# Three low parts per down stage move from a ScalarE copy and an accumulating transfer to one VectorE subtraction

## The reference

```
h = h + jnp.concatenate([y_lru, y_att], axis=-1) @ w_out[i]
u = rmsnorm(h, ln_ffn[i])
g_up, v_up = jnp.split(u @ w_up[i], 2, axis=-1)
g_up = causal_dwconv(g_up, ffn_conv_w[i], ffn_conv_b[i])
h = h + (jax.nn.gelu(g_up) * v_up) @ w_down[i]
gate = jax.nn.sigmoid(rmsnorm(h, ln_ple[i]) @ w_ple_gate[i])
h = h + gate * (p[i].astype(h.dtype) @ w_ple_proj[i])
```

## Time and profile before

| what | value |
|---|---|
| median of three runs | 634.01 us (633.53 to 634.43) |
| profiled execution, device time | 634.09 us |
| its span, first to last instruction | 632.3 us |
| TensorE | busy 627.9 us |
| VectorE | busy 438.4 us |
| ScalarE | busy 337.3 us |
| GpSimd | busy 362.1 us |
| granted TensorE clock | 1.000 |
| transfers of the software queue (only L563's) | 1296 packets, 4.72 MB |

### The profile page before, as it was taken

How to read it: one execution, slowest core, us unless ns; L and a number is a source line. 1 busy time by engine, 2 the same in 40 slices (tenths; PEclk the granted TensorE clock), 3 DMA queues, 4 the chain that set the end, 5 groups by cost and what they waited for, 6 DMA issues and landing times.

```text
span 632.3 us, 7947 instructions
## 1 busy us (share of the span) xinstructions
PE 627.9 (99%) x2885; PEld 521.5 (82%) x2885; DVE 438.4 (69%) x650; ACT 337.3 (53%) x492; POOL 362.1 (57%) x267
## 2 busy tenths in 40 slices
PE   9999999999999999999999999999999999999997
PEld 7887788888888888888888888888888888888886
DVE  3692499978748797769734477697354677989574
ACT  5779953878836455546333345453343364457341
POOL 6684433743307537499664454996644559963370
PEclk9999999999999999999999999999999999999999
DMA  8742335471103644303546223045462222652022
GB/s 297 289 136 98 101 100 133 123 203 61 41 1 121 242 171 167 100 1 102 132 137 233 97 100 101 1 119 128 154 230 76 99 95 93 170 172 100 34 84 83
DMA packets 22934, 77.80 MB, mean 123 GB/s; under 512 B 2672, under 2 KB 3184, under 8 KB 22640
## 3 DMA queue, kind: packets, MB, share of 16 engines
q1 hardware_dynamic: 21456, 72.45, 34.3%
q0 software_dynamic: 1296, 4.72, 4.0%
q10 hardware_dynamic: 144, 0.13, 0.1%
HBM read 64.83 MB, written 4.19 MB: 109 GB/s over the span
## 4 chain that ended last, share of the span: by engine, by line
PE 99%; DVE 0%; issue 0%; POOL 0%; POOLq 0%
PE psum L1519 30%; PE psum L1521 30%; PE psum L1520 30%; PE psum L1715 2%; PE psum L1701 1%; PE psum L1661 1%; PE psum L1565 1%; PE psum L1568 1%; PE psum L1573 1%; PE psum L1598 1%; PE psum L1848 1%; PE psum L1631 1%; PE psum L1616 1%; PE psum L1682 0%; PE psum L1558 0%; PE psum L1658 0%
## 5 line engine op out<-in xcount | busy, mean ns | idle before, releaser
L505 POOL TENSOR_TENSOR wlo<-raw,whi 128x512 fp32r<-128x512 f32 x82 | 112.9, 1377 | 192.3 <-ACT whi L591 191.9
L1521 PE MATMUL psum<-uhi,wlo 128*128 128x512 f32 x488 | 189.8, 389 | 0.0
L1520 PE MATMUL psum<-ulo,whi 128*128 128x512 f32 x488 | 189.8, 389 | 0.0
L1519 PE MATMUL psum<-uhi,whi 128*128 128x512 f32 x488 | 189.8, 389 | 0.0
L506 POOL TENSOR_TENSOR wlo<-raw,whi 128x512 fp32r<-128x512 f32 x82 | 117.6, 1434 | 0.0
L591 ACT ACTIVATE whi<-raw 128x1024 fp32r<-128x1024 f32 x78 | 81.9, 1054 | 58.0 <-PE psum L1521 57.3
L1520 PEld LDWEIGHTS psum<-ulo,whi 128*128 128x128 f32 x488 | 91.6, 188 | 19.1
L1519 PEld LDWEIGHTS psum<-uhi,whi 128*128 128x128 f32 x488 | 91.6, 188 | 19.1
L1521 PEld LDWEIGHTS psum<-uhi,wlo 128*128 128x128 f32 x488 | 91.6, 188 | 18.9
L837 ACT ACTIVATE tmp<-psum,vec 128x512 f32<-128x512 f32 x24 | 16.6, 690 | 84.3 <-DVE psum L1293 84.3
L1364 DVE TENSOR_TENSOR ws<-raw,held 128x1024 f32<-128x1024 f32 x24 | 47.1, 1987 | 9.3 <-POOL elo L557 9.1
(11 more groups left out here) (253 smaller groups left out, 1183.9 us busy)
## 6 DMA issues: line engine op xcount, KB each, us to landing
raw<-in_weights SPq DMA_DIRECT2D x94, 512.0 KB, 3.3
held<-in_weights SPq DMA_DIRECT2D x12, 512.0 KB, 5.7
wlo<-ws POOLq DMA_DIRECT2D x6, 512.0 KB, 5.9
xtok<-in_x SPq DMA_DIRECT2D x4, 512.0 KB, 8.8
out<-first SPq DMA_DIRECT2D x1, 2048.0 KB, 8.7
back<-out SPq DMA_DIRECT2D x1, 2048.0 KB, 7.7
first<-in_x_t SPq DMA_DIRECT2D x7, 256.0 KB, 7.1
raw<-in_weights SPq DMA_DIRECT2D x7, 256.0 KB, 7.1
```

Source lines behind the costliest of these rows:

```text
L505: nc.gpsimd.tensor_tensor(wlo[s][:, 0:CW // 2], raw[s][:, 0:CW // 2], whi[s][:, 0:CW // 2].bitcast(F32), ALU.subtract)
L1519: mm(o, ahi, bhi, start=start, stop=False, skip_group_check=shared)
L1520: mm(o, ahi, blo, start=False, stop=False, skip_group_check=shared)
L1521: return mm(o, alo, bhi, start=False, stop=stop, skip_group_check=shared)
```

## The change

The negated copy on ScalarE, the accumulating transfer and its semaphores go. A new helper own_low on VectorE subtracts the high part from the sum in ws for units 8, 10 and 12 and counts v_low. All that waited for x_low waits for v_low. VectorE's order changes: the three subtractions are put in, and sum 6 moves behind give 0.

```diff
             for ph in range(PHASES):
...
                 for u in range(N_UNITS):
-                    if u in ADDED:
-                        unit_add(ph, u)
-                    else:
+                    if u not in OWN:
                         unit_low(ph, u)
...
                 nc.scalar.activation(high[:, :], whole[:, :], ACT.Copy).then_inc(d_hi, 1)
-                if u in ADDED:
-                    act.wait_ge(d_hi, N_UNITS * ph + u + 1)
-                    nc.scalar.activation(low[:, :], high[:, :].bitcast(F32), ACT.Copy, scale=-1.0).then_inc(d_neg, 1)
...
                 elif n == 9:
-                    dve.wait_ge(x_low[8], 16 * (ph + 1))
+                    dve.wait_ge(v_low, len(OWN) * ph + 1)
...
+            def own_low(ph, u):
+
+                high, low = unit_slot(u)
+                dve.wait_ge(d_hi, N_UNITS * ph + u + 1)
+                V.tensor_tensor(low[:, :], ws[SUM_AT[SUM_UNITS.index(u)]][:, :], high[:, :].bitcast(F32), ALU.subtract).then_inc(v_low, 1)
...
+                own_low(ph, 8)
+                give(ph, 0)
                 weight_sum(ph, 6)
-                give(ph, 0)
                 weight_sum(ph, 7)
                 give(ph, 1)
+                own_low(ph, 10)
                 weight_sum(ph, 8)
                 weight_sum(ph, 9)
                 give(ph, 2)
+                own_low(ph, 12)
                 give(ph, 3)
                 give(ph, 4)
...
-                if u in ADDED:
-                    pe.wait_ge(x_low[u], 16 * (ph + 1))
+                if u in OWN:
+                    pe.wait_ge(v_low, len(OWN) * ph + OWN.index(u) + 1)
```

More of the change, by code:

```diff
@@ L136 @@
 PRODUCT_UNITS = [UNITS.index((o, 1)) + 1 for o in range(7)]
-ADDED = (8, 10, 12)
-LOW_UNITS = N_UNITS - len(ADDED)
+OWN = (8, 10, 12)
+LOW_UNITS = N_UNITS - len(OWN)
 SUM_UNITS = [u for u, (o, _) in enumerate(UNITS) if PRODUCTS[o][2] is not None]
@@ L163, in lows_upto @@
 def lows_upto(ph, u):
-    return LOW_UNITS * ph + u + 1 - sum(x < u for x in ADDED)
+    return LOW_UNITS * ph + u + 1 - sum(x < u for x in OWN)
 def after_down(c):
@@ L343, in build @@
         y_copy = sem("y_copy")
-        w_sum, d_hi, d_neg, d_lo, d_step = (sem(n) for n in ("w_sum", "d_hi", "d_neg", "d_lo", "d_step"))
-        x_low = {u: sem(f"x_low{u}") for u in ADDED}
+        w_sum, d_hi, v_low, d_lo, d_step = (sem(n) for n in ("w_sum", "d_hi", "v_low", "d_lo", "d_step"))
         unit_done, res_moved = sem("unit_done"), sem("res_moved")
@@ L558, in unit_low @@
                                         ALU.subtract).then_inc(d_lo, 1)
[L560 to L564, removed]
             for ph in range(PHASES):
@@ L835, in tap_up @@
                     else:
-                        act.wait_ge(x_low[12], 16 * (f // 8))
+                        act.wait_ge(v_low, len(OWN) * (f // 8))
                 nc.scalar.activation(ytile[f % 4], up_bank(f, 0), ACT.Identity, bias=0.0,
@@ L891, in square_ple @@
                 elif m == 0:
-                    act.wait_ge(x_low[12], 16 * PHASES)
+                    act.wait_ge(v_low, len(OWN) * PHASES)
                 elif m == 2:
@@ L1356, in weight_sum @@
                 elif n == 9:
-                    dve.wait_ge(x_low[8], 16 * (ph + 1))
+                    dve.wait_ge(v_low, len(OWN) * ph + 1)
                 elif ph and n == 0:
-                    dve.wait_ge(x_low[10], 16 * ph)
+                    dve.wait_ge(v_low, len(OWN) * ph)
                 elif ph:
```

## The result

| kernel | median us | runs | ratio to before, 95% interval |
|---|---|---|---|
| before | 633.97 | 633.53 to 634.43 (4) | |
| the change | 637.06 | 636.78 to 638.48 (4) | 1.0052 (1.004 to 1.0064) |

The change costs 3.1 us where 2.7 were forecast. The profiled execution is the slowest of the four (638.48 us, span 636.7): in it TensorE's clock fell for some microseconds after the longer wait. The other three lie between 636.8 and 637.2 us with spans of 635.0 to 635.4. One execution of the kernel with seven memsets (see the experiments) took 698.6 us at a mean granted clock of 0.851 and is left out of its numbers.

A forecast was written before the change was run, and what follows sets the result against it. TensorE, busy 99% of the span, bounds the kernel. Span 632.3 plus 2.7 us lateness at turn_back(4) gives 635.0; with 1.8 us around the span, 636.7 us against 634.01; range 634.4 to 638.6, forecast case's own 636.2 to 637.2.

The forecast's parts named there:

- What bounds: Whole span: TensorE is busy 99% and waits once, 1.0 us at the start; nothing the change removes stands on the path.
- Phases 0 and 1 covered: Phases 0 and 1: give 5 ends at 442.6, the next up tile comes at about 445.2; cover 2.6 us, no loss.
- The three subtractions: VectorE, phase 2: own_low(8), (10), (12) take 2.24, 1.35 and 1.22 us, cost 4.81; VectorE is 3.49 us late after give 4.
- the rival at 638.2: GpSimd goes first at own_low(12), where the margin is 0.21 us; add_back(0) starts 4.2 us late, 638.2 us; chance 20%.
- sharing at half speed: VectorE and GpSimd share SBUF at half speed instead of excluding each other: about +3.0 in place of +2.7 us; no chance given.
- pTlo blocked: VectorE, phase 2: the pTlo pair from 565.28 meets GpSimd's halves, lasts 3.0 us, not 1.29; add_back(0) at 568.19, 2.7 us late.
- From add_back(0) to give 6 as a block: Phase 2: everything from add_back(0) to give 6 moves together, so give 6 and turn_back(4) are 2.7 us late.
- The waits: TensorE waits twice after its start, near 564.8 (turn_back(0), about 0.8 us) and 575.4 (turn_back(4), about 1.9 us).
- The rival that the gap takes it: VectorE's 2.42 us gap before add_back(0) absorbs lateness, pTlo finding GpSimd idle: 635.1 us, or 634.0 at free pace; chance 17%.
- The rival that it gets faster: The 1.8 us around the span partly belong to the software queue and go; with no wait 632.2 us; chance 7%.

The follow-up runs named there:

- the kernel with seven memsets: The kernel before with seven memsets of acc on VectorE between give 4 and the pTlo pair of phase 2: 639.90 us, ratio 1.0089.
- The versions without the transfers and with no wait of TensorE: Give 6 ahead of low_ple, with the change plus pTlo on GpSimd and phase 2's own_low(12) behind give 4 (634.36 us), or all low parts on GpSimd (634.29).
- The kernel that holds GpSimd back: The changed kernel, with GpSimd waiting for the pTlo pair before the low part of the next stage's first chunk: 636.14 us, ratio 1.0035.
- The padded kernel: The kernel before with four memsets of acc on VectorE between give 4 and the pTlo pair of phase 2: 635.62 us, ratio 1.0025.

## Why the prediction was right, and where it was off

- **What bounds.** Right: no time came from what was removed. The versions without the transfers and with no wait of TensorE take the time of the kernel before (634.36 and 634.29 against 634.30).
- **Phases 0 and 1 covered.** Right, by the kernel with the change in these alone. Give 5 in phase 1 ended at 442.33 (forecast 442.6), the up tile came at 444.95 (445.2).
- **The three subtractions.** 2.31, 1.42 and 1.30 us, with 2.24, 1.35 and 1.22 forecast from start to start (544.07 to 546.31, 553.19 to 554.54, 560.30 to 561.52: 2.24, 1.35, 1.22). Give 3 was forecast at 561.70 and started at 561.52, which is 561.68 in the other execution's frame. own_low(12) won its turn, so the rival at 638.2 did not come; unit 13's second half took 2.28 us behind it. The prediction also named sharing at half speed, with about +3.0, which by the number alone is nearer to 3.1. These rows rule it out: own_low(12) had halves beside it all the time and at half speed would have taken, by estimate, nearly twice its free 1.13 us; it took 1.22.
- **pTlo blocked.** Right in place and size: 565.10 to 568.03, forecast 565.28 to 568.19 with the same 0.16 between the frames. The padded kernel shows the mechanism without the change. It is worth 2.7 us at add_back(0) together with the lateness, and 1.7 of them are the blocking: in the prediction's terms 3.49 - 2.42 = 1.07 from the lateness, the rest from the turns.
- **From add_back(0) to give 6 as a block.** This is the term that was mis-sized. add_back(0) is 2.7 us late, but give 6 is 2.95 (576.05 against 573.26 - 0.16). The neighbours did not move as one: low_ple(1) at 572.15 took 1.83 us, blocked by a half of the chunk after, and low_ple(2) at 575.38, blocked before (1.5 us from its start to give 6's), was free (0.67). From start to start the low_ple pair cost 1.1 us more (2.42 against 1.32) and low_ple(2) 0.8 less; that the two nearly cancel, and the block so came out within 0.3 us, is luck. The kernel that holds GpSimd back shows what these turns can do: it gains 1.7 us at add_back(0) and keeps 0.6 of them at give 6.
- **The waits.** Two, at turn_back(0) and turn_back(4), 0.6 and 2.1 us from starts where 0.8 and 1.9 were forecast. At the weight loads turn_back(0), whose first stood at 564.56 in the kernel before, is 565.24 - 564.56 + 0.16 = 0.8 us late and turn_back(4) 2.96.
- **The remaining 0.1 or so** between 2.95 and the measured 3.1 is within the measurement. Whether the clock has a part in it stays open: the timed runs carry only its mean (0.999, 1.000 and 0.999), and a mean of 0.999 also stands in a kernel where TensorE never waits (give 6 ahead of low_ple with all low parts on GpSimd).
- **The rival that the gap takes it** is out: the pair met the halves, and with four memsets a lateness of 0.2 us beyond the gap cost 1.6 us. **The rival that it gets faster** is out: the time around the span is 638.48 - 636.7 = 1.8 us, as before, though the software queue is gone.

## What to carry to other kernels

An engine at 99% of the span has no slack anywhere, so before work is given to another engine, look not at that engine's busy share (69% here) but at its list between two things the bound engine waits for: how much idle time it has there, and whether the margin at the second is zero. Count the instructions that read two SBUF operands on VectorE and lay GpSimd's beside them at the new times, those behind the inserted one too: a shift of 2.65 us against a gap of 2.42 cost 1.6 us here, not 0.2, as it moved a pair onto GpSimd's halves. And order the list so that what the bound engine waits for comes ahead of what it does not yet need.

## What the runs showed of the hardware

**TensorE's clock after a wait.** In the profiled execution of the kernel after, TensorE stood still for 2 us before 577.38. The windows of that execution (us; busy time and instructions of PE, PEld, DVE, ACT, POOL; the granted clock; DMA share, GB/s):

```profile
570.00:575.00 5.00, 5.00 (x23) 4.14 (x23) 5.00 (x6) 2.45 (x5) 2.85 (x2) 1.00 0.30 105
575.00:577.00 2.00, 0.43 (x2) 0.01 (x1) 1.80 (x4) 2.00 (x4) 0.16 (x2) 1.00 0.41 150
577.00:579.00 2.00, 1.62 (x9) 1.62 (x10) 2.00 (x3) 1.90 (x4) 2.00 (x2) 0.65 0.28 113
579.00:581.00 2.00, 2.00 (x10) 2.00 (x9) 1.81 (x4) 1.33 (x2) 0.94 (x1) 0.50 0.10 16
581.00:583.00 2.00, 2.00 (x10) 1.59 (x10) 2.00 (x4) 0.88 (x2) 0.00 (x0) 0.99 0.73 246
```

The granted clock was 0.50 (1.2 GHz in place of 2.4) from shortly after the wait to about 581. The 16 transposes and what followed them took 580.54 - 577.38 = 3.16 us to the next matmul; in the kernel before the same took 576.40 - 574.74 = 1.66. That is 1.5 us, and 638.48 - 637.06 = 1.4 is what this execution lies above the median. The profiled execution with the change in phase 2 only did the same (638.39 us, span 636.6, 0.50 from 579 to 581). By their times (636.8 to 637.2) the three other executions of each of the two kernels did not. The profiles with waits of 0.4 to 1.4 us after the start show 1.00 in every stretch from 560 to 583 us. With seven memsets and 3.8 us of waits all executions took 639.3 us or more; the profile shows 0.50 too, and its time is 1.8 us above what the lateness of give 6 explains. So in this kernel a wait of TensorE near 2 us cost 1.5 us more than itself in two executions and not in six others.

**Turns between VectorE and GpSimd.** In every kernel here the engine that waited went next, down to a lead of 0.18 us (own_low(12) at 560.30 against the half at 560.48, which then took 2.28 us). Memsets on VectorE and operations with one SBUF operand did not hold a half up: beside memsets and beside gives, halves take 1.28 to 1.30 us.
